# Reordering VectorE's queue in the first block of a two-block transformer on one core

## The reference

```
x = layer_norm(x)
for l in 0, 1:
    proj = x @ w_in[l]                       # heads of three attentions, low-rank latents, gate_pre
    na_out  = neighbourhood_attention(...)   # 8 heads, biased scores
    df_out  = diff_attention(...)            # 4 heads; p1 - lambda * p2, then rms_norm
    mla_out = latent_attention(...)          # q, k, v from normed latents; rotary parts; 8 heads
    merged  = g0 * (na_out @ wb0) + g1 * (df_out @ wb1) + g2 * (mla_out @ wb2)   # g = sigmoid(gate_pre + b)
    x = layer_norm(ALPHA * x + merged @ w_out[l])
    x = layer_norm(ALPHA * x + (silu(gate) * up) @ w_ffn_out[l])
```

## Time and profile before

| what | value |
|---|---|
| median of 3 runs | 1531.62 us (1529.98 to 1533.11) |
| profiled execution, its own time | 1531.43 us |
| span in the profile | 1530.0 us |
| PE busy | 1471.4 us (96%) |
| DVE, ACT busy | 1006.3 us (66%), 788.9 us (52%) |
| mean granted TensorE clock | 0.996 |

### The profile page before, as it was taken

One profiled execution on the slowest core, in us unless ns is written; L12 is line 12 of the kernel. 1 busy time (PEld: TensorE's weight loads), 2 busy tenths in 40 slices (PEclk: granted clock), 3 DMA queues, 4 the chain that ended last, 5 costly groups with the idle time before them and its releaser, 6 DMA issues.

```text
span 1530.0 us, 18329 instructions
## 1 busy us (share of the span) xinstructions
PE 1471.4 (96%) x7161; PEld 1204.7 (79%) x7161; DVE 1006.3 (66%) x1349; ACT 788.9 (52%) x1122; POOL 68.3 (4%) x100
## 2 busy tenths in 40 slices
PE   5999999899999999999999999999999999999998
PEld 4788787778887787787778887777888877778887
DVE  5565885765547655785774555877777767767675
ACT  3564654344343555655343443675655657765663
POOL 1000000000001000000010000210000011000000
PEclk9999999999999999999999999999999999999999
DMA  9544653566564544552666565436465544445551
GB/s 312 178 146 136 210 174 100 190 194 202 186 214 141 209 140 143 179 164 85 192 218 192 168 202 180 131 101 206 151 201 175 188 142 163 141 158 197 166 176 72
DMA packets 167317, 260.99 MB, mean 171 GB/s; under 512 B 8768, under 2 KB 106720, under 8 KB 166720
## 3 DMA queue, kind: packets, MB, share of 16 engines
q1 hardware_dynamic: 166048, 252.03, 50.8%
q0 software_dynamic: 896, 6.74, 1.2%
q10 hardware_dynamic: 288, 1.05, 0.2%
HBM read 258.74 MB, written 1.05 MB: 170 GB/s over the span
## 4 chain that ended last, share of the span: by engine, by line
PE 85%; DVE 8%; ACT 4%; issue 2%; POOL 1%; DMA 1%; SPq 0%; ACTq 0%; DVEq 0%
PE ps L382 14%; PE ps L386 14%; PE ps L384 14%; PE ps L455 11%; PE ps L457 11%; PE ps L456 11%; DVE wlo L1444 2%; PE ps L522 1%; PE ps L966 1%; ACT whi L1023 1%; PE ps L532 1%; PE ps L509 1%; PE ps L703 1%; DVE proj L2008 1%; PE ps L412 1%
## 5 line engine op out<-in xcount | busy, mean ns | idle before, releaser
L1444 DVE TENSOR_TENSOR wlo<-raw,whi 128x2048 fp32r<-128x2048 f32 (+1 forms) x238 | 528.6, 2230 | 280.4 <-ACT whi L1023 280.1
L1023 ACT ACTIVATE whi<-raw 128x2048 fp32r<-128x2048 f32 (+1 forms) x238 | 441.6, 1866 | 210.0 <-PE ps L386 112.1
L382 PE MATMUL ps<-whi,xTh 128*128 128x512 f32 x704 | 278.1, 395 | 6.1 <-DVE wlo L1444 2.4
L386 PE MATMUL ps<-whi,xTl 128*128 128x512 f32 x704 | 274.7, 390 | 0.0
L384 PE MATMUL ps<-wlo,xTh 128*128 128x512 f32 x704 | 274.5, 390 | 0.0
L455 PE MATMUL ps<-whi,xTh 128*128 128x512 f32 (+3 forms) x640 | 253.4, 396 | 9.9 <-DVE xTl L1470 3.2
L457 PE MATMUL ps<-whi,xTl 128*128 128x512 f32 (+3 forms) x640 | 244.6, 382 | 0.0
L456 PE MATMUL ps<-wlo,xTh 128*128 128x512 f32 (+3 forms) x640 | 243.9, 381 | 0.0
L382 PEld LDWEIGHTS ps<-whi,xTh 128*128 128x128 f32 x704 | 132.3, 188 | 35.1 <-DVE wlo L1444 3.2
L386 PEld LDWEIGHTS ps<-whi,xTl 128*128 128x128 f32 x704 | 132.2, 188 | 27.9
L384 PEld LDWEIGHTS ps<-wlo,xTh 128*128 128x128 f32 x704 | 132.4, 188 | 26.3
(11 more groups left out here) (184 smaller groups left out, 1632.8 us busy)
## 6 DMA issues: line engine op xcount, KB each, us to landing
raw<-in_w_in SPq DMA_DIRECT2D x124, 512.0 KB, 4.6
raw<-in_w_ffn_in SPq DMA_DIRECT2D x88, 512.0 KB, 4.9
raw<-in_w_up SPq DMA_DIRECT2D x88, 512.0 KB, 4.9
raw<-in_w_ffn_out SPq DMA_DIRECT2D x44, 512.0 KB, 4.5
raw<-in_w_down SPq DMA_DIRECT2D x44, 512.0 KB, 4.7
raw<-in_w_branch SPq DMA_DIRECT2D x24, 512.0 KB, 4.6
raw<-in_w_out SPq DMA_DIRECT2D x16, 512.0 KB, 4.4
raw<-in_w_o SPq DMA_DIRECT2D x16, 512.0 KB, 4.7
```

Source lines behind the costliest of these rows:

```text
L382: PE.matmul(o, ah, hi[:, j, b], start=first and kt == 0, stop=False)
L386: mm = PE.matmul(o, al, hi[:, j, b], start=False, stop=last and j == c - 1 and i == len(kts) - 1)
L1023: AC.activation(m.whi[:, i % SPLIT, 0:w], m.raw[:, slot, 0:w], ACT.Copy).then_inc(s.w_hi, 1)
L1444: DV.tensor_tensor(m.wlo[:, i % SPLIT, 0:w], m.raw[:, slot, 0:w], m.whi[:, i % SPLIT, 0:w].bitcast(F32), ALU.subtract).then_inc(s.w_lo, 1)
```

## The change

It only moves work in the queues of VectorE and, at one place, of ScalarE. TensorE's program and the loads are as before.

```diff
 ScalarE, df stage, each g:
             if g:
                 probs_out(p0, g - 1, 0)
+            split_to(k.seen[1, L, "df", g, 2][0] + SPLIT)
             catch(1, L, "df", g, 3)
 VectorE, evict of a branch half:
             DV.scalar_tensor_tensor(out=g, in0=g, scalar=1.0, in1=o, op0=ALU.add, op1=ALU.mult).then_inc(free, 1)
-            if (i, j) == (0, 0):
-                rotate_latent(L, th)
 VectorE, na stage:
-            catch(1, L, "na", g, 1)
+            catch(1, L, "na", g, 1, ahead=0 if g else SPLIT)
 VectorE, df stage:
             if g:
                 subtract_pair(h0, g - 1)
             if g < 3:
                 qk_out(P, (g + 1) % 2)
-            catch(1, L, "df", g, 1)
-            catch(1, L, "df", g, 2)
+            if g == 4:
+                for part in range(2):
+                    rotate_latent(L, part)
+            catch(1, L, "df", g, 1, ahead=0 if g else SPLIT)
+            catch(1, L, "df", g, 2, ahead=0 if g else SPLIT)
+            split_to(k.seen[1, L, "df", g, 2][0] + SPLIT)
             catch(1, L, "df", g, 3, ahead=SPLIT - 1)
 VectorE, ml stage:
-            catch(1, L, "ml", g, 1)
+            catch(1, L, "ml", g, 1, ahead=0 if g else SPLIT)
 VectorE, w stage:
-        catch(1, L, "w", 0)
-        catch(1, L, "w", 1)
+        w0 = k.first[1, L, "w", 0]
+        catch(1, L, "w", 0, ahead=0)
+        split_to(w0 + 1)
+        catch(1, L, "w", 1, ahead=0)
         turn_lo_quarter(0, 0, 0.5)
-        catch(1, L, "w", 2)
-        for th, n4 in ((1, 0), (0, 1), (1, 1)):
-            turn_lo_quarter(th, n4, 0.5)
+        catch(1, L, "w", 2, ahead=0)
+        turn_lo_quarter(1, 0, 0.5)
+        turn_lo_quarter(0, 1, 0.5)
+        split_to(w0 + 2)
+        turn_lo_quarter(1, 1, 0.5)
         catch(1, L, "w", 3)
```

## The result

The changed kernel takes 1543.5 us (median of 6 runs, 1542.1 to 1544.43) against 1531.62 us for the kernel before (6 runs, 1529.98 to 1533.31): ratio 1.0075 [1.0062, 1.0088], slower by 11.9 us. The profiled execution took 1544.43 us with a span of 1543.0, against 1531.43 and 1530.0 of before, so the two traces that are compared differ by 13.0 us. The forecast was 1540.0 with a range of 1533.8 to 1546.0.

A forecast was written before the change was run, and what follows sets the result against it. TensorE's stops were taken to bound the kernel. The w stage costing 15.8 us and the df stage gaining 6.8 gave +9.0 on 1531.43, 1540.4, stated as 1540; range 1533.8 to 1546, the forecast's own 1536 to 1543.

The forecast's parts named there:

- What bounds the kernel: Whole kernel: PE is busy 1471.4 of 1530.0 us, so only TensorE standing still more or less moves the end.
- three kinds of wait: TensorE waits, each once per layer: for the merged sum 5.1 us, the subtraction 4.1, the copied values 2.8; 12.0 in all.
- The df stage: VectorE's and ScalarE's new order removes waits of 1.39, 0.15 and 1.89 us: gain 3.4 a layer, 6.8 in both.
- the bank: df stage: a branch 0 sum must free the bank the first gate half uses at 178.9, 0.5 us to spare.
- The w stage, first half: First w product: the 3.1 us wait becomes 5.5 before piece 39, early start given back, +0.2 us a layer.
- The w stage, second half: Start of the second w product: pieces 40 and 41 follow the eviction, so TensorE stands 3.9 us a layer.
- The clock: Behind both new w-stage waits TensorE runs at 1.2 GHz: 1.7 us each, plus 0.3 for a turning; bounds 0 to 1.7 each.
- The sum: Whole kernel: w stage 7.9 us a layer, 15.8 in both, less 6.8 from df, together +9.0 us.
- (b): df stage gains nothing because rotation, bank, q and k copy or key copies come late: 1547.4 us, half 1544; chance 0.14.
- (a): w stage: the clock stays up after the new waits, sum +2.2, 1533.8 us; chance 0.08.
- (c): w stage: piece 40 is subtracted before the first w product ends, old waits and slow blocks go, 1516.4 us; chance 0.05.
- (d): Whole kernel: other waits of the same size replace each removed one, 1531.6 us; chance 0.03.

The follow-up runs named there:

- The two kernels above: Changed kernel with the earlier w list, plus either the latent rotation put back (1526.37 us) or ScalarE's added df rounding taken out (1528.44 us).
- the kernel with added products: Changed kernel plus matmuls nobody reads, into a free PSUM bank, ahead of TensorE's two new w-stage waits: 1533.46 us.
- the version without either stop: Changed kernel with pieces 37 to 41 subtracted earlier and ScalarE rounding the quarters before piece 41: 1515.33 us.

## Why the prediction was right, and where a size was off

**What bounds the kernel: right.** Only TensorE's stops and its clock moved the end. The three kinds of wait of the earlier trace rows went as the prediction said.

**The df stage: right, 3.4 forecast, 3.9 measured at the start of the ml stage.** The named waits make 3.43, and some 0.4 more were idle time with no name around them, so the bound "3.43 at most" was too low. The two kernels above show that each edit did its own part. Of the margins that the prediction listed, the rotation (forecast 174.1 to 177.8, measured 173.92 to 177.7) and the bank were kept; the copy of q and k with "nothing to spare" was indeed late by 0.3 us. In the ml stage 0.26 went at one turning of probabilities (forecast 0, bounds 0 to 0.9). The kernel with only the df edits arrives at the w stage 3.6 us earlier than before, so the na and ml edits give back 0.5 a layer. What arrives at the w stage is 3.1 a layer instead of 3.4.

**The w stage, first half: right.** The working had TensorE go on at 277.05 on the clock of the trace before. It went on at 273.95, which is 277.02 on that clock, since it came 3.07 us earlier. The wait stands at the turning (L412) ahead of that product, not at L455, for which the prediction had looked. That the early start is given back whole, because piece 39 stands behind a load that nobody moved, is shown by the kernel in which ScalarE turns the rows first: there the wait is 1.27.

**The w stage, second half: right.** 3.9 forecast, 3.79 measured, in both layers and in each kernel that kept this order, and gone when pieces 40 and 41 stood ahead of the eviction.

**The clock: the mechanism right, the size too small.** This is the term of the sum that was mis-sized. The prediction gave both stops the slow stretch of the wait of before, 1.7 each, with 0.3 for the turning and 0.1 for a slow start: 3.8 a layer. Measured are 0.4 + 2.3 + 2.9 = 5.6 in layer 0 and 5.4 in layer 1. Before, a part of the products behind the wait still ran at the upper level (PEclk 0.66 over five microseconds); after, all of them did at the lower for 5 to 5.7 us (0.50 in both windows). The stretch was taken from a stop of another length, and no row of before showed what follows a longer one. The net price was further off than its size: the slow products of before cost next to nothing, as the last section shows, and those of the changed kernel cost 10 us. The price of 0 to 1.7 for each, called bounds, was no upper bound.

**The sum.** Forecast +9.0 in the traces. The clock adds 1.8 + 1.6 = 3.4, the smaller gain ahead of w 0.6, and the second wait takes 0.2 off: 12.8 of the 13.0 us by which the spans differ. With the right clock term the sum would have been 1531.43 + 9.0 + 3.4 = 1543.8, by a profiled execution of 1544.43. The measured 1543.5 lies 0.5 above the forecast's own range, 1536 to 1543. It lies inside the stated one because rival (b), which did not happen, carried the upper end to 1546, not because the clock's price had been given room. That the range held is luck in this respect.

**The rivals.** (a), the clock stays up, was wrong for this kernel, but the kernel with added products is this case, and it took 1533.46 us where the prediction worked out 1533.8. (b), the df stage gains nothing, is out: its lists alone give 7 to 9 us. (c) was reached by the version without either stop, 1515.33, which needs one more edit at each stop, and earlier splits in the ml stage. (d) is out: the new waits are not of the size of the old.

The Trainium skill's page "TensorE: Matmul & The Clock Gate", section "Why this matters for your kernels", with its advice to keep idle gaps under about 3 us, puts the new stops of both layers (5.10 and 3.79, 4.09 and 3.79) on the side that is punished. In the trace of the changed kernel all four were; other runs agree with it only in part, as the last section shows.

## What to carry to other kernels

Where work is moved ahead in an in-order queue, look first at what it waits for: here two small roundings were moved ahead of a split, they stood behind another engine's load, and the split was held by it. A helper that evicts and then prepares operands ties the next product to the end of the one before; whoever takes preparation out of its early place must put it ahead of the eviction. And price a stop of TensorE as its idle time plus the slow products behind it, which here was 2.7 us on top of 3.8. Do not take that price from a shorter stop, and ask whether the next operand would have been late anyway: then slow products cost nothing.

## What the runs showed of the hardware

The clock behind a stop is not a fixed function of its length. A stop of 1.99 us in layer 1 was followed by the lower level in the kernel before and in the one with only its w list put back, and not in three others with the same list (rotation back, no added rounding, df edits only). A stop of 3.06 us in layer 0 was followed by it in all but one of these. Behind a stop of 3.79 us the first product took 0.77 us in the changed kernel, and 0.47 in the kernel with the w list alone, which slowed down 1.3 us later. What decides between them stays open. It is not what TensorE did just ahead of the stop: in the 12 us ahead of the 1.99 us stop, and of the 3.06 us stop, its matmuls start at the same distances from the stop in all five traces, within 0.02 us.

The df stage shows it too. The kernel before did not slow down behind its wait of 1.89 us for the subtraction. The kernel with only the new w list has the df stage of before, and its trace has the lower clock behind this wait in both layers, in layer 1 from 1.4 us later on. In layer 0:

```profile
176.99 0.66 PE L522 MATMUL ps<-ident,prob 128*128 128x128 f32 x4 [1.85 <-DVE prob L1647]
177.40 0.59 PE L455 MATMUL ps<-whi,aTh 128*128 128x512 f32 x1
177.79 0.63 PE L456 MATMUL ps<-wlo,aTh 128*128 128x512 f32 x1
```

Near the start of the kernel, where no edit reaches, TensorE waits at 29.0 to 29.4 us for a split. In five of the twelve traces (before, changed, and those with pieces 40 and 41 first, turned rows first, and neither stop) this wait is 2.6 to 2.9 us and the lower clock follows it; in the other seven it is 1.5 to 2.4 and does not. So the same point of the df stage lies at 158.1 to 158.6 in the five and at 156.6 to 157.0 in the seven. The rows are from the changed kernel and from the one with added products:

```profile
29.17 0.50 PE L455 MATMUL ps<-whi,xTh 128*128 128x512 f32 x1 [2.66 <-DVE wlo L1445]
```

```profile
29.09 0.50 PE L464 MATMUL ps<-whi,xTh 128*128 128x512 f32 x1 [1.90 <-DVE wlo L1454]
```

Two traces can thus differ by 1 to 2 us ahead of any changed stage, and a single stage has to be measured from a point just ahead of it. It also means that a difference of under 2 us between two kernels above (1.7, 1.8) is not certain in its size.

Nor were the slow products of before worth their 1.7 us. Where the clock stayed up behind the wait for the sum, TensorE stood 1.2 us further on, for a rounded quarter. These are the turning and the product behind this second wait in layer 1, of the kernel with only the df edits (clock up) and then the product of the kernel before (clock down), whose turning is at 740.03:

```profile
731.47 0.66 PE L412 MATMUL ps<-ident,gate 128*128 128x128 f32 x4 [1.99 <-DVE gate L1555]
...
736.80 0.50 PE L455 MATMUL ps<-whi,xTh 128*128 128x512 f32 x1 [1.21 <-DVE xTl L1471]
```

```profile
745.38 0.48 PE L455 MATMUL ps<-whi,xTh 128*128 128x512 f32 x1
```

It is 5.33 us in the one and 5.35 in the other, and the whole w stage of layer 1 takes 31.2 us in all five traces, whatever the clock. So the lower clock cost nothing there: slow products used up time in which the quarter would have been waited for. Behind the new stops nothing waited further on, and the clock cost its full price.
